# The start of a transformer block on one Trainium2 core: z, values and dt in one pass with the tokens stationary

## The reference, cut to what matters

```
h = rms_norm(x, norm_mix_w[i])                      # x: 512 tokens x 1024
proj = einsum("bld,de->ble", h, w_in[i])            # 1024 -> 2320 columns
q, k, v, z, xbc_raw, dt_raw = split(proj, [512, 640, 768, 1280, 2304])
...
dt = softplus(dt_raw + dt_bias)                     # 16 columns, scan
y = y * silu(z)                                     # gate of the scan, 512 columns
```

## Time and profile before

| | |
|---|---|
| median of 3 runs | 2722.69 us |
| profiled execution: its time, its span | 2721.53 us, 2719.7 us |
| PE busy | 2688.3 us (99%) |
| PE weight loads | 2179.8 us (80%), beside PE |
| DVE, ACT busy | 1512.5 us (56%), 1158.6 us (43%) |
| granted PE clock | 0.999 of full |
| DMA moved | 256.47 MB, 94 GB/s on average |

### The profile page before, as it was taken

One profiled execution on the slowest core, in us unless ns is written; L12 is line 12 of the kernel. 1 busy time (PEld: TensorE's weight loads), 2 busy tenths in 40 slices (PEclk: granted clock), 3 DMA queues, 4 the chain that ended last, 5 costly groups with the idle time before them and its releaser, 6 DMA issues.

```text
span 2719.7 us, 33585 instructions
## 1 busy us (share of the span) xinstructions
PE 2688.3 (99%) x13780; PEld 2179.8 (80%) x13780; DVE 1512.5 (56%) x2109; ACT 1158.6 (43%) x1690; POOL 25.6 (1%) x45
## 2 busy tenths in 40 slices
PE   9999999999999999999999999999999999999998
PEld 7767888888767888888888888887777888888887
DVE  6685444345685444344443346688788864544433
ACT  6774322225774322233222234455588463422221
POOL 0000000000000000000000000000000000000000
PEclk9999999999999999999999999999999999999999
DMA  6202332334202332332333342222223332333222
GB/s 222 76 18 94 102 100 94 98 95 147 78 17 93 101 101 93 94 100 93 101 94 95 99 139 82 78 71 70 84 76 105 126 96 96 94 101 93 97 93 66
DMA packets 75369, 256.47 MB, mean 94 GB/s; under 512 B 9040, under 2 KB 12240, under 8 KB 74832
## 3 DMA queue, kind: packets, MB, share of 16 engines
q1 hardware_dynamic: 72704, 241.21, 28.1%
q0 software_dynamic: 2512, 13.11, 1.3%
HBM read 242.22 MB, written 8.39 MB: 92 GB/s over the span
## 4 chain that ended last, share of the span: by engine, by line
PE 92%; ACT 4%; DVE 3%; issue 0%; DMA 0%; SPq 0%; DVEq 0%; ACTq 0%
PE PS L1422 27%; PE PS L1424 27%; PE PS L1423 27%; PE PS L1381 1%; PE PS L1625 1%; PE PS L1444 1%; PE PS L1445 1%; PE PS L1446 1%; PE PS L1592 1%; PE PS L1607 1%; ACT PT L1907 1%; DVE WLO L2110 0%; ACT DE L1863 0%; PE PS L1571 0%; PE PS L1671 0%
## 5 line engine op out<-in xcount | busy, mean ns | idle before, releaser
L1422 PE MATMUL PS<-HHI,WHI 128*128 128x512 f32 x2288 | 909.3, 397 | 0.0
L1424 PE MATMUL PS<-HHI,WLO 128*128 128x512 f32 x2288 | 891.4, 390 | 0.0
L1423 PE MATMUL PS<-HLO,WHI 128*128 128x512 f32 x2288 | 890.9, 389 | 0.0
L2110 DVE TENSOR_TENSOR WLO<-WR,WHI 128x1024 fp32r<-128x1024 f32 (+2 forms) x446 | 536.0, 1204 | 509.1 <-ACT WHI L1713 506.0
L1713 ACT CAST WHI<-WR 128x1024 fp32r<-128x1024 f32 (+2 forms) x446 | 457.8, 1027 | 430.4 <-PE PS L1424 406.5
L1422 PEld LDWEIGHTS PS<-HHI,WHI 128*128 128x128 f32 x2288 | 429.5, 188 | 100.5 <-issue 12.5
L1423 PEld LDWEIGHTS PS<-HLO,WHI 128*128 128x128 f32 x2288 | 429.8, 188 | 90.6 <-issue 4.6
L1424 PEld LDWEIGHTS PS<-HHI,WLO 128*128 128x128 f32 x2288 | 429.4, 188 | 90.8
L1422 PE MATMUL PS<-FHI,WHI 128*128 128x512 f32 x682 | 265.3, 389 | 0.0
L1423 PE MATMUL PS<-FLO,WHI 128*128 128x512 f32 x682 | 265.3, 389 | 0.0
L1424 PE MATMUL PS<-FHI,WLO 128*128 128x512 f32 x682 | 265.3, 389 | 0.0
(11 more groups left out here) (341 smaller groups left out, 2586.3 us busy)
## 6 DMA issues: line engine op xcount, KB each, us to landing
WR<-in_stream SPq DMA_DIRECT2D x413, 512.0 KB, 3.5
WR<-in_stream SPq DMA_DIRECT2D x32, 384.0 KB, 3.1
xkeep<-X POOLq DMA_DIRECT2D x3, 2048.0 KB, 8.1
X<-xkeep POOLq DMA_DIRECT2D x24, 256.0 KB, 5.1
ROT<-RQ SPq DMA_DIRECT2D x40, 64.0 KB, 2.0
X<-in_xin SPq DMA_DIRECT2D x8, 256.0 KB, 6.8
out<-X SPq DMA_DIRECT2D x8, 256.0 KB, 2.2
KD<-RQ SPq DMA_DIRECT2D x8, 128.0 KB, 3.8
```

Source lines behind the costliest of these rows:

```text
L1422: e.matmul(out, hi[:, i, :], xhi, start=first, stop=False)
L1423: e.matmul(out, hi[:, i, :], xlo, start=False, stop=False)
L1424: t = e.matmul(out, lo[:, i, :], xhi, start=False, stop=final)
L2110: e.tensor_tensor(lo, raw, hi.bitcast(F32), ALU.subtract).then_inc(S["dve_low"], 1)
```

## The change

The columns of z, v and dt (512 + 128 + 16 = 656) become slots of one row of 656 columns each (eight a layer). `product_wide` streams them past the stationary x tiles: per row and chunk three times one matmul of 400 columns into the chunk's own bank, and one of 256 columns (112 of z, the 128 of v, the 16 of dt) into half of a "rest" bank, which two chunks share. The group of dt and v, their transposes and their copies go. ACT copies dt out of the two rest banks, applies Silu to each chunk in two pieces (400 and 112 columns), and scales v out of the rest banks. A bank of z is now evicted only once both chunks that share a rest bank are done. The rescaling moves into the pass (RESCALED says after which row and chunk). At the start x rows and slots alternate one by one, and there is no half slot. At the end of the kernel, the first half's `hsum` is planned 1.6 us later, and `hsq` counts as a step of the log/exp table.

```diff
+TOKEN_COLUMNS = np.concatenate([np.arange(768, 1280), np.arange(640, 768), np.arange(2304, 2320)])
+WIDE = 400
+RESCALED = ({(5, 3): 0, (6, 1): 2, (6, 3): 4, (7, 3): 6}, {(3, 3): 0, (5, 1): 2, (6, 3): 4, (7, 3): 6})
...
     down = ((0, 8), (8, 8), (16, 6))
     for l in range(2):
-        tm("w_in", l, 768)
-        fm("w_in", l, 2192)
-        fm("w_in", l, 640)
+        for r in range(DT):
+            s.append(("w_in", l, r, 1, 640, len(TOKEN_COLUMNS)))
         for c in IN_ORDER:
...
 FUNCTIONS = {
-    **dict.fromkeys("root hroot rroot dta ex dexp gsq exp small rln dd eb roroot ldecay llog lmult croot".split(), LOG_EXP),
+    **dict.fromkeys("root hroot hsq rroot dta ex dexp gsq exp small rln dd eb roroot ldecay llog lmult croot".split(), LOG_EXP),
...
+    def chunk(self, p, c):
+        if c == CH - 1:
+            self.release()
+        else:
+            self.tokens += 1
+            self.token[p, c] = self.tokens
+
+    def product_wide(self, p, rhs, name, i, c0, rescaled):
+
+        self.rhs[p] = rhs
+        for c in range(CH):
+            self.take((*p, c))
+        for b in range(CH // 2):
+            self.take((*p, "rest", b), "side")
+        for r in range(DT):
+            k = self.slot(name, i, r, c0)
+            self.slot_of[p, r] = k
+            for c in range(CH):
+                self.add("zrow", p, r, c)
+                self.chunk(p, c)
+                self.beat()
+                if (r, c) in rescaled:
+                    self.rescale(rhs[1], p, rescaled[r, c])
+        self.final[p] = k
 
...
-            self.after["hhi", m, j] = (p, r0)
+            self.after["hhi", m, j] = (p, j if (p, j) in self.slot_of else r0)
...
+        if h == 0:
+            yield 1.6
         yield self.add("hsum", h)
...
-        self.product_tokens(("z", l), ("U", 2 * l), "w_in", l, 768)
+        z = ("z", l)
+        self.product_wide(z, ("U", 2 * l), "w_in", l, 640, RESCALED[l])
         self.add("qns", l)
+        dt = self.add("dt", l)
         for c in range(CH):
-            self.free(("z", l, c), ("act_zsilu", self.add("zsilu", l, c)))
+            self.free((*z, c), ("act_zsilu", self.add("zsilu", l, c)))
+        v = self.add("v", l)
+        for b in range(CH // 2):
+            self.free((*z, "rest", b), ("act_zsilu", ("zsilu", l, 2 * b + 1)), ("act_v", v), ("act_dt", dt))
         def raw(t, c0):
             self.product(("raw", l, t), ("H", 2 * l), "w_in", l, c0)
             taken(t)
 
         def taken(t):
-            first = {4: ("dtT", l), 5: ("vT", l), 6: ("kdup", l)}.get(t)
...
+            if t == 6:
+                self.run(lambda: ("kdup", l) in self.n)
             self.free(("raw", l, t), ("act_raw", self.add("raw", l, t)))
 
         self.ring.update(main=(4, 5, 6), side=(0, 1, 2, 3, 7))
-        for chain in (self.dt_tokens, self.v_tokens, self.to_tokens, self.ssd_states, self.attention):
+        for chain in (self.to_tokens, self.ssd_states, self.attention):
             self.spawn(chain(l))
-        self.product_group(("U", 2 * l), [(("raw", l, 0), "w_in", l, 2192), (("raw", l, 1), "w_in", l, 640)], rescaled=2 * l)
...
-        self.add("xin", 0)
-        self.add("load0")
-        self.add("xin", 1)
-        self.load()
-        for j in range(2, DT, 2):
+        for j in range(DT):
             self.add("xin", j)
             self.load()
-            self.add("xin", j + 1)
...
-        self.next_split = SPL
-        for _ in range(RAW):
+            if j < SPL + 2:
+                self.add("high", j)
+            self.add("ulo", 0, j)
+            if j < SPL + 2:
+                self.low[j] = self.add("low", j)
+            if j > 0:
+                self.add("sq", 0, j - 1)
+            if j > 1:
+                self.add("acc", 0, j - 1)
+        self.add("sq", 0, DT - 1)
+        self.add("acc", 0, DT - 1)
+        self.next_split = SPL + 2
+        for _ in range(2):
...
+            elif kind == "zrow":
+                p, r, c = a
+                k = o.slot_of[p, r]
+                hi, lo = (w[:, 0, :] for w in weights(k))
+                out, rest = PS[o.bank[*p, c]][:, 0:WIDE], PS[o.bank[*p, "rest", c // 2]]
+                rest = rest[:, 256 * (c % 2):256 * (c % 2) + 256]
+                if r == 0:
+                    emptied(q, (*p, c))
+                    if c % 2 == 0:
+                        emptied(q, (*p, "rest", c // 2))
+                if c == 0:
+                    weights_split(q, k)
+                q.wait_ge(S["dve_ulo"], n["ulo", o.rhs[p][1], r])
+                xhi, xlo = HHI[:, r, c * P:(c + 1) * P], HLO[:, r, c * P:(c + 1) * P]
+                kw = {"skip_group_check": True}
+                e.matmul(out, xhi, hi[:, 0:WIDE], start=r == 0, stop=False)
+                e.matmul(rest, xhi, hi[:, WIDE:], start=r == 0 and c % 2 == 0, stop=False, **kw)
+                e.matmul(out, xhi, lo[:, 0:WIDE], start=False, stop=False)
+                e.matmul(rest, xhi, lo[:, WIDE:], start=False, stop=False, **kw)
+                e.matmul(out, xlo, hi[:, 0:WIDE], start=False, stop=r == DT - 1)
+                t = e.matmul(rest, xlo, hi[:, WIDE:], start=False, stop=r == DT - 1 and c % 2 == 1, **kw)
                 t.then_inc(S["pe_slot" if c == CH - 1 else "pe_token"], 1)
...
                 q.wait_ge(S["dve_scale"], n["scale", m, j])
-                if m == 6:
-                    q.wait_ge(S["pe_slot"], o.slot_of[o.after[step]] + 1)
-                elif j < DT - 2:
-                    q.wait_ge(S["pe_urow"], 3 * (m // 2) + j // 2 + 1)
-                else:
-                    q.wait_ge(S["pe_slot"], o.final["raw", m // 2, 1] + 1)
+                q.wait_ge(S["pe_slot"], o.slot_of[o.after[step]] + 1)
...
                     q.wait_ge(s_spill, 16 * (l + 1))
-                done_chunk(q, ("z", l), c)
+                done_chunk(q, ("z", l), c | 1)
                 q.wait_ge(S["act_rooted"], n["root", 2 * l])
-                e.activation(Z[:, c, :], PS[o.bank["z", l, c]][:, :], ACT.Silu, scale=RSC[:, c:c + 1]).then_inc(S["act_zsilu"], 1)
+                rest = PS[o.bank["z", l, "rest", c // 2]][:, 256 * (c % 2):256 * (c % 2) + T - WIDE]
+                e.activation(Z[:, c, 0:WIDE], PS[o.bank["z", l, c]][:, 0:WIDE], ACT.Silu, scale=RSC[:, c:c + 1])
+                e.activation(Z[:, c, WIDE:T], rest, ACT.Silu, scale=RSC[:, c:c + 1]).then_inc(S["act_zsilu"], 1)
+            elif kind == "dt":
+                l, = a
+                done(q, ("z", l))
+                for b in range(CH // 2):
+                    rest = PS[o.bank["z", l, "rest", b]][:, :].rearrange("p (c t) -> p c t", c=2)
+                    t = e.copy(DTR[:, 2 * b:2 * b + 2, :], rest[:, :, 240:256])
+                t.then_inc(S["act_dt"], 1)
             elif kind == "conv0":
                 l, j = a
...
                 l, = a
-                q.wait_ge(S["pe_turn"], n["vT", l])
...
                 for c in range(CH):
-                    t = e.activation(V[:, c, :], PS[o.bank["vT", l]][:, c * P:(c + 1) * P], ACT.Copy, scale=RSC[:, c:c + 1])
+                    at_ = 256 * (c % 2) + T - WIDE
+                    t = e.activation(V[:, c, :], PS[o.bank["z", l, "rest", c // 2]][:, at_:at_ + P], ACT.Copy, scale=RSC[:, c:c + 1])
...
                 q.wait_ge(S["act_rooted"], n["root", 2 * l])
                 for c in range(CH):
-                    t = e.scalar_tensor_tensor(DTR[:, c, :], PS[o.bank["dtT", l]][:, c * P + 112:c * P + 128], RSC[:, c:c + 1],
+                    t = e.scalar_tensor_tensor(DTR[:, c, :], DTR[:, c, :], RSC[:, c:c + 1],
```

More of the change, by code:

```diff
@@ L367, in product_group @@
                 self.beat()
-            if rescaled is not None and r % 2:
-                self.rescale(rescaled, p, r - 1)
     def product_tokens(self, p, rhs, name, i, c0, rescaled=None):
-        self.rhs[p], self.token[p] = rhs, len(self.token)
+        self.rhs[p] = rhs
         for c in range(CH):
@@ L634, in to_tokens @@
             self.free(("bT", l, h), ("act_bt", self.add("bt", l, h)))
-    def dt_tokens(self, l):
-        yield from self.until(("raw", l, 0))
-        yield from self.room()
-        self.take(("dtT", l), "side")
-        yield self.add("dtT", l)
-        self.free(("dtT", l), ("dve_dt", self.add("dt", l)))
-    def v_tokens(self, l):
-        yield from self.until(("raw", l, 1))
-        yield from self.room()
-        self.take(("vT", l), "side")
-        yield self.add("vT", l)
-        self.free(("vT", l), ("act_v", self.add("v", l)))
     def ssd_states(self, l):
@@ L1301, in slot_tiles @@
     def slot_tiles(k):
-        part = slice(0 if k else 512, o.slots[k][3] * o.slots[k][5])
+        part = slice(0, o.slots[k][3] * o.slots[k][5])
         return WR[:, k % RAW, part], WHI[:, k % SPL, part], WLO[:, k % SPL, part]
@@ L1426, in tensor_engine @@
                     t.then_inc(S["pe_slot"], 1)
-                elif p[0] == "raw" and p[2] == 1 and r % 2:
-                    t.then_inc(S["pe_urow"], 1)
             elif kind == "trow":
```

(20 more changed lines are left out.)

60 lines of the change are left out of this document (17 added, 43 removed), and 6 rows, old and new, of the table TIMES.

## The result

The changed kernel takes 2735.59 us (median of 6 runs, 2734.34 to 2736.03) against 2722.71 (2722.23 to 2723.09) for the kernel before beside it: ratio 1.0049, 95% interval 1.0039 to 1.0059. It is 13 us slower. I had forecast 2719.3 with 2711.5 to 2727.5; the result lies outside, and on the other side.

The account below looks back on a forecast made before the run. PE, busy 99% of the span, was taken to bound the kernel. Layer 0 2.7, layer 1 2.25, attention -2.0 and end 0.5 sum to 3.4 us less: 2722.69 becomes 2719.3 us, range 2711.5 to 2727.5 (8 in 10).

Parts of the forecast that it names:

- The matmuls: Product pass, per layer: 28.8 us added for 32.7 removed gains 3.9; transposes gone 1.36; together 5.25 us.
- Rival C: Product pass: 256-column matmuls bound by their weight loads, 0.19 instead of 0.120 us each: 2732.7 us; chance 0.02.
- The start: First layer's start: idle before row 1 goes, 1.84 us gained; wider first slot costs 0.4; PE starts about 7.05.
- Behind the pass in layer 0: Layer 0's first products: waits of 0.9 us at row 6 and 4.6 us for the second product's bank.
- The idle at row 6: Layer 0, first product: PE waits 0.9 us until row 6 of H is rescaled.
- The wait for the keys: Layer 0, first attention step: its 1.46 us idle for copied keys goes, 1.5 us more gain, 2.7 in all.
- Layer 1: Layer 1's pass and products: 5.25 us saved, less 0.2 and a 2.8 us wait at the second product: gain 2.25.
- The attention: Between last product and output product: one pair step more costs 1 us a layer, 2.0 in the sum.
- The end: Kernel's end: fifteen matmuls ahead of the first half's `hsum` cover its 0.35 us idle; gain 0.5 us.
- B: Tenth pair sets the attention's length, 7.5 us a layer: 2729.9 us, chance 0.10; mark: stretch over 75 us.
- the four cases: Bank wait mostly absent (0.28), tenth pair sets attention (0.10), loads bind narrow matmuls (0.02), forecast's own mechanism (0.60).

Follow-up runs that it names:

- e2: Kernel before, attention pairs behind the last product started 6.3 instead of 6.0 us apart by the planner's clock: 2733.52 us, ratio 1.0046.
- e3: Changed kernel, attention pairs behind the last product started 6.6 instead of 6.0 us apart: 2725.42 us, ratio 1.0015.
- e9: Changed kernel with bank 7 for the second product, pairs 6.6 us apart behind the last product, each layer's first pair 2 us later: 2714.34 us, ratio 0.9973.
- e1: Changed kernel with bank 7 given to the second product, every engine's order kept: 2732.69 us, ratio 1.0044.
- e11: Kernel before with only the change's two edits for the end of the program: 2722.03 us, ratio 0.9999.
- e6: Kernel before, seventh attention pair held until the last product, so ten pairs behind it instead of nine: 2736.51 us, ratio 1.0054.
- e7: Kernel before, seventh pair held until the last product (ten pairs behind it) and pairs 6.6 instead of 6.0 us apart: 2729.45 us, ratio 1.0027.
- e10: Kernel before, no new pair while chunk 1's decays wait for banks, pairs 5.2 us apart behind the last product: 2721.13 us, ratio 0.9998.
- e13: Kernel before with the output product's weight splits ordered earlier, behind the third chunk's token product: 2721.86 us, ratio 1.0001.

## Why the prediction was wrong

**The matmuls: right.** From the timeline of PE in the new pass (start, length, operation):

```profile
8.79 0.35 PE L1464 MATMUL PS<-WHI,HHI 128*128 128x400 f32 x1
8.98 0.28 PE L1465 MATMUL PS<-WHI,HHI 128*128 128x256 f32 x1
9.10 0.34 PE L1466 MATMUL PS<-WLO,HHI 128*128 128x400 f32 x1
```

A pair takes 0.31 us here (0.30 on average over the pass), and the pass from 7.78 to the first product at 38.46, 30.7 us, where 28.8 + 1.75 were predicted. Rival C falls, and with it, for these loads, the sentence of the Trainium skill ("TensorE: Matmul & The Clock Gate", section The mechanism) by which a load overlaps running matmuls only where the row groups differ. The same section also lets a load into a background weight buffer run ahead; whether that is the case here no run shows.

**The start: direction right, size off.** No idle before row 1. PE starts at 7.78, not 7.05: the first low part of weights is late by 1.34 us of idle, so the wider first slot and the new order of the loads, which no run takes apart, cost 1.1 us, where I charged 0.4 (0.2 to 0.8).

**Behind the pass in layer 0: right but for the clock.** The idle at row 6 is 0.64 us (0.9 predicted). ACT's list in front of the second product:

```profile
43.15 0.27 ACT L1811 COPY DTR<-PS 128x32 f32<-128x32 f32 x2
43.43 1.28 ACT L1804 ACT_TABLE_LOAD   x1
44.73 0.59 ACT L1804 ACTIVATE Z<-PS,RSC 128x400 f32<-128x400 f32 x1
45.22 0.35 ACT L1805 ACTIVATE Z<-PS,RSC 128x112 f32<-128x112 f32 x1
...
47.59 1.19 ACT L1833 ACTIVATE V<-PS,RSC 128x128 f32<-128x128 f32 x4
```

It takes 48.78 - 43.15 = 5.6 us (6.0 predicted). The Silu starts right behind the table load, so there is no room for a drain here either. The Trainium skill ("ScalarE: Activation LUTs", section What ACT_TABLE_LOAD costs) gives a drain of about 1.38 us with each load of another table; the trace does not agree. PE and what follows its wait, the first of each three matmuls:

```profile
48.88 0.47 PE L1427 MATMUL PS<-HHI,WHI 128*128 128x512 f32 x1 [3.84 <-issue]
...
50.47 0.63 PE L1427 MATMUL PS<-HHI,WHI 128*128 128x512 f32 x1
51.75 0.63 PE L1427 MATMUL PS<-HHI,WHI 128*128 128x512 f32 x1
53.03 0.63 PE L1427 MATMUL PS<-HHI,WHI 128*128 128x512 f32 x1
53.99 0.39 PE L1427 MATMUL PS<-HHI,WHI 128*128 128x512 f32 x1
```

The wait is 3.84 us (4.6 predicted), the bank free within 0.3 us of my time. The profile names no releaser for it ("issue"), but PE starts 0.1 us behind the end of the scaling of v, 48.78, the last eviction in its list of waits. But from about 50.1 to 53.6 three matmuls take 1.28 us instead of 0.68: the lower of the clock's two levels, 1.7 us lost. I had priced a wait at its length. The wait for the keys is gone in this layer, as predicted.

**Layer 1: right.** Wait of 2.13 us at the second product (2.8 predicted), none at row 6, full clock there. One wait of 0.9 us for keys that I had not seen (I had said that there would be none).

**The attention: this step failed.** "I take 1 us a layer", within bounds of nothing and 7.5 us less the pair's PE work of 2 to 3 us, so 5.5 at most. The tails grew by 10.7 and 12.1 us. Of this 4.9 and 3.1 us are PE work that moved in, which is no loss by itself, as the products end earlier by it. What is left, 5.8 and 9.0 us, is to be held against the 1 us, and lies beyond the upper bound in both layers: 4.1 and 5.9 us of idle time (10.7 us of idle instead of 6.6 in layer 0) and 1.6 and 3.1 us of clock, 14.7 us where 2.0 were in the sum. The step assumed that the tail keeps its order and gets one pair more. But nobody keeps it: the planner lays it out anew from where its clock stands, by greedy rules with free banks as their currency, and the order before was a good one (e2: one number moved by 5% costs 11.8 us). The pair is at most a small part: e3 and e9 keep the same pairs, and e9's tails of 71 us are only 2.8 us longer than before with 3.7 to 4.5 us more PE work in them. The stalls ahead are not the main part either (e1, e3). Which of the moved steps costs how much stays open. The prediction counted what was left for the tail, and not in which sequence the scan's chunks came there.

**The end: right.** 0.6 us (0.5 predicted), confirmed by e11.

**The rivals.** B's mark (a stretch over 75 us) is met, but its mechanism is not the cause: a redrawn order lengthens the stretch just as well, so the mark could not tell the two apart. Nor is any of the four cases: the case that an order made by rules is redrawn for the worse was missing from the list, and it needs a chance wherever a planner sits behind a change.

## What to carry to other kernels

Where a greedy planner writes the order, a change that saves work upstream also redraws everything behind it: compare the sequence of the dependent chain at the end of the stretch and not only the counts, and treat the old order as tuned: here the redraws of the order before lost (e2, e6, e7 and the change itself) or changed nothing (e10, e13). Try such a change with two or three settings of the planner before judging it. A wait of TensorE can cost more than its length, since the clock may fall behind it, and removing one wait brings out the next (here the bank, then the keys, then the weight split), so look for them together.

## What the hardware showed that I had not expected

Most stretches at the lower clock in these traces are about 4 us long and cost 1.4 to 1.7 us (four ran to 8 us and cost 2.5 to 3.1). Those that I looked at lie behind waits of TensorE: 3.84 us in the changed kernel, 2.16 us for keys in e1, 2.14 us for weights in e9. But the length of the wait does not tell whether one comes: the 2.13 us wait in layer 1 of the changed kernel was followed by none, nor was the wait of 2.49 us in layer 0 of e9. The start of the kernel before shows the same. It had none in spite of a wait of 1.67 us near 9 us; in e13, which starts in the same way, the wait was 2.37 us and there was none either, but in e2, e6, e7, e10 and e11, with that start too and waits of 1.81 to 2.13 us, there was one between 9 and 14 us, of 1.5 to 1.7 us. So the same sequence comes with it or without. That would fit the spread of the kernel before, 2719.8 to 2724.7 us in the last set of runs, but only one of its executions was traced. The new pass has no such wait at the start, and none of its eight traces shows a lower clock there. What decides it these runs do not show.
